# Expert weights in a hybrid SSD / gMLP / MoE step: chunks of one row step of both experts, and extra steps taken row by row in the doubled pair

## The reference

```
for each expert e:                      # w_gu[e] 1024 x 2048, w_down[e] 1024 x 1024, all float32
    gu = x[tokens of e] @ w_gu[e] + b_gu[e]
    act = glu * sigmoid(1.702 * glu) * (lin + 1)      # glu, lin: clamped even and odd columns
    y[tokens of e] += gate * (act @ w_down[e] + b_down[e])
```

## Time and profile before

| | us |
|---|---|
| runs of the kernel before | 1468.93, 1472.8, 1466.63 (median 1468.93) |
| the profiled execution's own time | 1467.76 |
| its span, first to last instruction | 1465.6 |
| PE busy in the span | 1389.4 (95%) |
| packets of the SP queue, share of 16 DMA engines | 77.7% |
| mean granted TensorE clock | 0.99 |

### The profile page before, as it was taken

One profiled execution on the slowest core, in us unless ns is written; L12 is line 12 of the kernel. 1 busy time (PEld: TensorE's weight loads), 2 busy tenths in 40 slices (PEclk: granted clock), 3 DMA queues, 4 the chain that ended last, 5 costly groups with the idle time before them and its releaser, 6 DMA issues.

```text
span 1465.6 us, 21942 instructions
## 1 busy us (share of the span) xinstructions
PE 1389.4 (95%) x8524; PEld 815.9 (56%) x8525; DVE 585.9 (40%) x1304; ACT 381.3 (26%) x643; POOL 206.9 (14%) x305
## 2 busy tenths in 40 slices
PE   7999999999999999999899899999999989889996
PEld 6998888888999444434434345343443443434432
DVE  6788887877443254312312123131221231212214
ACT  5557777766322241001001000010100100100002
POOL 4034454536810000000000000000000000000000
PEclk9999999999999999999999999999999999999999
DMA  8434555555454789999999999999999999999996
GB/s 263 133 121 151 150 178 153 173 169 147 158 158 144 316 344 386 428 429 429 428 428 429 429 428 426 429 427 386 424 428 428 429 428 429 429 428 428 428 424 235
DMA packets 124889, 482.91 MB, mean 330 GB/s; under 512 B 7197, under 2 KB 95325, under 8 KB 99929
## 3 DMA queue, kind: packets, MB, share of 16 engines
q1 hardware_dynamic: 86752, 459.16, 77.7%
q10 hardware_dynamic: 35904, 18.88, 4.4%
q0 software_dynamic: 2160, 3.87, 0.8%
HBM read 470.55 MB, written 11.34 MB: 329 GB/s over the span
## 4 chain that ended last, share of the span: by engine, by line
PE 69%; DMA 23%; DVE 3%; ACT 2%; issue 1%; SPq 1%; POOL 1%; ACTq 0%; POOLq 0%; DVEq 0%
DMA ring_b<-in_w_gu 19%; PE bank L1482 18%; PE bank L1688 11%; PE bank L1291 8%; PE bank L970 4%; PE bank L961 4%; PE bank L1409 4%; PE bank L942 3%; DMA ring<-in_w_gu 3%; PE bank L966 2%; PE bank L963 2%; PE bank L1520 2%; PE bank L1310 2%; PE bank L1200 1%; PE bank L1570 1%
## 5 line engine op out<-in xcount | busy, mean ns | idle before, releaser
L1482 PE MATMUL bank<-ring_b,xe 128*64 128x512 f32 x1168 | 324.1, 613 | 38.2 <-DMA ring_b<-in_w_gu 30.0
L1482 PEld LDWEIGHTS bank<-ring_b,xe 128*64 128x64 f32 x1168 | 103.7, 141 | 234.3 <-issue 233.5
L1482 PE MATMUL bank<-ring,xe 128*64 128x512 f32 x720 | 215.5, 596 | 3.1 <-DMA ring<-in_w_gu 3.1
L1688 PE MATMUL bank<-ring,actT 128*64 128x512 f32 x672 | 198.6, 595 | 0.0
L1821 ACT ACTIVATE swi<-swi 128x256 f32<-128x256 f32 x65 | 27.0, 417 | 549.0 <-DVE swi L2805 518.2
L2846 DVE TENSOR_TENSOR hid<-hid,bank 128x512 f32<-128x512 f32 (+1 forms) x90 | 57.7, 681 | 225.6 <-PE bank L1434 207.8
L1291 PE MATMUL bank<-rounded,ring_r 128*128 128x320 f32 x912 | 133.7, 307 | 1.7 <-DVE ring_r L2628 1.7
L1291 PEld LDWEIGHTS bank<-rounded,ring_r 128*128 128x128 f32 x912 | 132.8, 188 | 2.6 <-DVE ring_r L2628 2.4
L914 POOL TENSOR_TENSOR kept<-take 128x256 bf16<-128x256 bf16 x15 | 9.2, 612 | 829.6 <-PE bank L1670 829.6
L1482 PEld LDWEIGHTS bank<-ring,xe 128*64 128x64 f32 x720 | 68.4, 137 | 64.7 <-issue 64.7
L1688 PE MATMUL bank<-ring_b,actT 128*64 128x512 f32 x224 | 98.7, 594 | 4.0 <-ACT actT L2204 4.0
(11 more groups left out here) (421 smaller groups left out, 2026.6 us busy)
## 6 DMA issues: line engine op xcount, KB each, us to landing
ring_b<-in_w_gu SPq DMA_DIRECT2D x76, 2048.0 KB, 16.6
ring<-in_w_gu SPq DMA_DIRECT2D x48, 2048.0 KB, 16.7
ring<-in_w_down SPq DMA_DIRECT2D x45, 2048.0 KB, 18.1
ring<-in_w_in SPq DMA_DIRECT2D x32, 1024.0 KB, 5.4
ring_b<-in_w_down SPq DMA_DIRECT2D x15, 2048.0 KB, 15.8
arena<-in_state_ssm ACTq DMA_DIRECT2D x16, 512.0 KB, 4.9
out<-arena ACTq DMA_DIRECT2D x16, 512.0 KB, 3.6
ring<-in_w_branch_ssd SPq DMA_DIRECT2D x8, 1024.0 KB, 5.1
```

Of the source, the lines that this page charges most:

```text
L1482: mm = pe.matmul(bank[q][side(h), :], xe[:, j, side(h)], moe_slot(2 * i + h, first)[:, 2 * FF * k + 512 * q:2 * FF * k + 512 * q + 512], s ...
L1688: mm = pe.matmul(bank[4 + half][side(h), :], actT[:, f, side(h)], w[:, D * k + 512 * half:D * k + 512 * half + 512], start=False, stop=(f ...
```

## The change

A chunk still has 2 MB and a pair still has twelve, but a chunk of `w_gu` is now one row step of both experts, and a chunk of `w_down` two steps f of both. It is loaded by two DMAs of 1 MB, each of 2048 consecutive floats (8 KB) in 128 partitions, `PIECE` floats apart in the slot. PE waits for one chunk at each row step and gives it back at its end. In the doubled pair, the extra steps of rows 0 and 1 stay together; from row 2 to row 5 each row step is followed at once by its extra step; the extra steps of rows 6 and 7 come after row 7. Chunks there are given back after the extra step. In the last pair only chunks 10 and 11 are still special, and keep their layout (`LAST_WHOLE` = 10).

```diff
-LAST_WHOLE = 2 * GU_CHUNKS - 2
+LAST_WHOLE = PAIR_CHUNKS - 2
+PIECE = GU_ROWS * FF
 def pair_chunk_ready(pe, n, c, more16, first=False):
-            count = n * 32 + (filled[s] + 16 * (c // MOE_RING + 1))
+            count = n * 64 + (filled[s] + 32 * (c // MOE_RING + 1))
 ...
-            def load_chunk(c, e, j, first=False):
-                    sp.dma_start(dst, gu_t[j][:, bass.ds(e, 1), :].rearrange("p e n -> p (e n)")
+            def load_chunk(c, experts, first=False):
+                rows_t, i = (gu_t, c) if c < KD else (down_t, c - KD)
+                at = slice(PIECE * (i % 2), PIECE * (i % 2) + PIECE)
+                for h in range(2):
+                    sp.dma_start(dst[:, PIECE * h:PIECE * h + PIECE],
+                                 rows_t[i // 2][:, bass.ds(experts[h], 1), at].rearrange("p e n -> p (e n)")
+                                 ).then_inc(full, 16)
 ...
 def gate_up(...):
-                    elif k == 0:
-                        for h in range(2):
-                            pair_chunk_ready(pe, n, 2 * i + h, more16, first)
+                    pair_chunk_ready(pe, n, j, more16, first)
                     for q in range(4):
                         for h in range(2):
 ...
-                            if q == 3 and k == GU_ROWS - 1:
-                                mm.then_inc(chunk_used, 1)
+                    mm.then_inc(chunk_used, 1)
 def gate_up_double(n):
-                for i in range(GU_CHUNKS):
-                    both(2 * i)
-                    both(2 * i + 1)
-                    if i < 3:
-                        combine(n - 1, i)
-                    if i == 0:
+                for j in range(KD):
+                    both(j)
+                    if j in (1, 3, 5):
+                        combine(n - 1, j // 2)
+                    if j == 1:
 ...
-                    more_slots(2 * i)
-                    more_slots(2 * i + 1)
+                        more_slots(0)
+                    if 1 <= j < KD - 2:
+                        more_slots(j)
+                more_slots(KD - 2)
+                more_slots(KD - 1)
 def down_double(n):       # more_slots(j), four steps f
-                    mm.then_inc(chunk_used, 1)
+                        if f % 2 == 1:
+                            mm.then_inc(chunk_used, 1)
```

More of the change, by code:

```diff
@@ L1455, in combine_last, with gate_up @@
                               start=False, stop=True).then_inc(S["cm_psum"], 1)
[L1457 removed]
+            def gate_up(n, more16, first=False, before_it=False, extras=None, double=False, inputs=False):
                 if first:
@@ L1560, in both @@
                 def both(f):
[L1562 to L1566, removed]
+                    if f % 2 == 0:
+                        pair_chunk_ready(pe, n, KD + f // 2, None)
+                    if f % DOWN_ROWS == 0:
+                        pe.wait_ge(S["at_ready"], 2 * n + (f // DOWN_ROWS + 1))
                     for half in range(2):
                         for h in range(2):
[L1569 to L1574, removed]
+                            pe.matmul(bank[4 + half][side(h), :], actT[:, f, side(h)], down_row(f, h, half),
+                                      start=False, stop=(f == KD - 1))
                 def more_slots(j):
-                    for k in range(DOWN_ROWS):
-                        f = DOWN_ROWS * j + k
+                    for f in range(DOWN_ROWS * j, DOWN_ROWS * j + DOWN_ROWS):
                         for half in range(2):
[L1581 to L1584, removed]
+                            mm = pe.matmul(bank[3][quarter(2 * half + f % 2), :], actT_extra[:, f, :],
+                                           down_row(f, 1, half), start=(f == 1), stop=(f >= KD - 2))
+                        if f % 2 == 1:
+                            mm.then_inc(chunk_used, 1)
                 for f in range(DOWN_ROWS):
@@ L1626, in down_last @@
                 turn_half(0)
[L1627 to L1631, removed]
-                        mm = pe.matmul(bank[4 + half][side(h), :], actT[:, f, side(h)],
-                                       w[:, D * k + 512 * half:D * k + 512 * half + 512],
-                                       start=False, stop=(f == KD - 1))
-                    return mm
                 pe.wait_ge(S["at_ready"], 2 * n + 1)
                 for piece in range(2):
-                    for h in range(2):
-                        last_piece_ready(pe, 2 * GU_CHUNKS + h, piece, more16)
+                    pair_chunk_ready(pe, n, KD + piece, more16)
                     for f in (2 * piece, 2 * piece + 1):
                         for half in range(2):
-                            mm = down_step(f, half)
+                            for h in range(2):
+                                mm = pe.matmul(bank[4 + half][side(h), :], actT[:, f, side(h)], down_row(f, h, half),
+                                               start=False, stop=False)
                     mm.then_inc(chunk_used, 1)
@@ L1653, in down_last @@
                     for h in range(2):
-                        last_piece_ready(pe, 2 * (GU_CHUNKS + 1) + h, half, more16)
+                        last_piece_ready(pe, LAST_WHOLE + h, half, more16)
                     for f in range(DOWN_ROWS, KD):
-                        mm = down_step(f, half)
+                        at = D * (f - DOWN_ROWS) + 512 * half
+                        for h in range(2):
+                            mm = pe.matmul(bank[4 + half][side(h), :], actT[:, f, side(h)],
+                                           moe_slot(LAST_WHOLE + h)[:, at:at + 512], start=False, stop=(f == KD - 1))
                     mm.then_inc(chunk_used, 1)
@@ L1676, in down @@
                 for f in range(KD):
-                    j, k = f // DOWN_ROWS, f % DOWN_ROWS
-                    if k == 0:
-                        for h in range(2):
-                            pair_chunk_ready(pe, n, 2 * (GU_CHUNKS + j) + h, more16, first)
+                    if f % 2 == 0:
+                        pair_chunk_ready(pe, n, KD + f // 2, more16, first)
                     if f % 4 == 0:
@@ L1686, in down @@
                         for h in range(2):
-                            w = moe_slot(2 * (GU_CHUNKS + j) + h, first)
-                            mm = pe.matmul(bank[4 + half][side(h), :], actT[:, f, side(h)],
-                                           w[:, D * k + 512 * half:D * k + 512 * half + 512],
+                            mm = pe.matmul(bank[4 + half][side(h), :], actT[:, f, side(h)], down_row(f, h, half, first),
                                            start=False, stop=(f == KD - 1))
-                            if k == DOWN_ROWS - 1 and half == 1:
-                                mm.then_inc(chunk_used, 1)
+                    if f % 2 == 1:
+                        mm.then_inc(chunk_used, 1)
                     if f == 3 and first:
@@ L1810, in _ @@
                 block_of(n, more * 16, extras=more)
-            gate_up(NP - 1, more * 16, before_it=True, last=True, extras=more)
+            gate_up(NP - 1, more * 16, before_it=True, extras=more)
             down_last(more * 16)
```

99 lines of the change are left out of this document (40 added, 59 removed).

## The result

The changed kernel takes 1474.61 us in the median of 12 runs (1473.32 to 1478.96), the kernel before 1468.88 (1466.63 to 1472.82, 12 runs). The ratio is 1.0043, with a 95% interval of 1.0034 to 1.0052: some 6 us slower, within the 0.5% that was named as no telling change, though the interval shows that it is not zero. The profiled execution has a span of 1471.9 us, against 1465.6.

What follows compares the result with a forecast made beforehand. Transfers, not PE, were taken to set the pace: 192 chunks plus a tail. +13.0 - 3.55 - 4.4, with 0 for the ends, gave +5.05 us on the median 1468.93: forecast 1474 (chance 0.54), range 1464 to 1486.

Steps and rivals of the forecast that it cites:

- term 3: Doubled pair: the stream's stop for lack of free slots goes away with finer give-backs, -4.4 us.
- Term 1: Steady stream: 8 KB loads lower the rate to 422 GB/s, 0.0755 us more for each of 172 chunks, +13.0 us.
- Rivals A: Stream rate: it costs more, 417 GB/s, +23.2 - 8 = +15, 1484, slower; chance 0.24.
- C: Steady stage: 8 KB costs nothing, rate stays at 428 GB/s, -8 us, 1461, faster; chance 0.10.
- rival D: Stream: each added DMA leaves the engines idle for a moment; 0.3 us of it would give 1518; chance 0.01.
- Term 2: Start: an earlier give-back in pair 0 lets chunk 2 of pair 1 issue sooner, -3.55 us.
- Term 4: The ends: loads ahead of the router, the last pair's halves and all behind the last landing change nothing, 0.
- Rival B: Doubled pair: it keeps its gap, give-back too late or PE not ahead, +9.5 us, 1478.4, slower; chance 0.11.

Runs made afterwards that it cites:

- e1: Kernel before, each chunk loaded by two DMAs of 8 KB runs, waits and give-backs untouched: 1477.9 us, ratio 1.0076.
- e3: Kernel before, each w_gu chunk in one DMA with two 8 KB runs per partition, row steps reordered: 1475.05 us, ratio 1.0043.
- e10: Changed kernel with pair 0 back in one-expert chunks (one DMA, 16 KB runs): 1477.71 us, ratio 1.0064 to the kernel before.
- e5: Kernel before with only pair 0 in row-step chunks of both experts (two DMAs, 8 KB runs): 1467.1 us, ratio 1.000.
- e4: Changed kernel with the old order of extra steps in the doubled pair: 1475.16 us, ratio 1.0046 to the kernel before.
- e7: Changed kernel, row-step chunks only in pairs 0, 7, 8 and from row 6 of the last; 16 KB runs elsewhere: 1467.79 us, 0.9993 to the kernel before.
- e8: Changed kernel, row-step chunks only in pairs 0, 1, 6, 7, 8 and from row 6 of the last: 1465.6 us, 0.9979 to the kernel before.
- e2: Kernel before, each chunk loaded by two DMAs of 64 partitions, runs still 16 KB: 2162.3 us, no ratio given.

## Why the prediction was right

**The size and the sign.** 1474 was predicted and 1474.61 measured. That it is so close is partly luck: term 3 earned 1.0 us less than forecast and 1.0 us was lost at a place that had been put at nothing, while the medians lie only 0.7 us further apart than forecast (5.7 against 5.05).

**Term 1, +13.0, held.** 422 GB/s in all windows of whole pairs, 4.970 us a chunk in the chain, from eight halves of the last pair. e1 shows that it is the runs of the load and not the new waits, e3 that it is their length and not the number of DMAs. Rivals A (417) and C (428) fall, and with them D. The Trainium skill's numbers for a single DMA of 1 MB (DMA: Bandwidth & Descriptors, Bandwidth) played no part in a queue that is never empty: 186 more DMAs left no cost that is seen beside that of the runs. The "over +1200 us" of the prediction takes the Trainium skill's 6.15 us for one DMA of 1 MB (same page and section). By the 341 GB/s of the same row two of 1 MB take 6.15 us together, and the sum would be about +210 us, an estimate from that row. Nothing of either size came.

The 1518 of rival D does not follow from its 0.3 us, since 172 x 0.3 is 51.6 us: 1526 on top of the forecast, or 1513 in place of its rate. Nothing else rests on it.

**Term 2, -3.55, held as the changed kernel has it** (3.59 in the traces of e10 and of the changed kernel). But its reason was incomplete. I took it as a property of pair 0 alone. (567.71, which it gave for the issue of chunk 2, is that of chunk 3, but the sum uses the give-back at 567.35.) e5 shows that it also takes pair 1's give-backs by row, or a stream that is slower: with whole chunks behind it the stream loses 2.0 us again.

**Term 3, -4.4, was 1.0 us too large, and most of what it earned comes with the slower stream alone.** Between the landings at row 5 of pair 6 and row 7 of pair 9 lie 38 chunks. The kernel before takes 190.98 us for them, 5.0 over full rate. The changed kernel takes 1075.86 - 885.33 = 190.53, which is 1.6 over 38 x 4.970 = 188.9. So 3.4 are gained, not 4.4. In e1, with the old give-backs, the chain has the same two landings:

```profile
889.31 7.09 PE bank L1487 x32
...
1080.59 7.11 PE bank L1487 x32
```

191.28, only 2.4 over full rate. So with the slower stream taken first, 2.6 of the 3.4 us come from it, which asks for its slots later, and 0.8 from finer chunks. No run has finer chunks there without the lower rate, so the shares in the other order are open. A stop of a stream that waits for PE is a part of PE's time, and any slowing of the stream fills it first. I had named this (the give-backs hardly move in pair 7), but did not take it for the main cause.

**Term 4, nothing at the ends, missed 1 us in the last pair.** From row 7 of pair 9 to the last landing the kernel before takes 373.18 us and the changed one 379.42, so 6.24 more, where term 1 has 70 x 0.0755 = 5.3. The chain of the changed kernel from row 7 of pair 14 on, and the last landing of the kernel before:

```profile
1374.10 3.65 PE bank L1473 x16
...
1424.82 3.68 PE bank L1473 x16
...
1440.82 14.46 DMA ring<-in_w_down
```

```profile
1435.10 13.89 DMA ring<-in_w_down
```

From 1374.10 to row 5 of pair 15 at 1424.82 are ten chunks, which take 50.72 us instead of 49.70. The two other kernels with fine chunks at the start of the last pair have this too (51.17 in e4, 50.63 in e10), e1 has not (49.89). Why this landing is late is open.

**The sum.** Counted from the first row step of pair 0, the landing at row 5 of pair 6 comes 0.92 us later than in the kernel before (1.3 by terms 1 and 2), the 38 chunks of term 3 take 0.45 less (1.5 forecast), and the rest takes 6.24 more (5.3). That makes +6.7, less 0.4 by which the mixer ended earlier in this execution: 6.3, the difference of the two spans. The medians differ by 5.7.

**Rival B and DVE.** Rival B (the gap stays) did not come, but its place was rightly named: e7 and e8 have the stop there. DVE's later `swiglu` was hidden, as said; its idle time before the next work fell from 2.64 us to 1.62 in the changed kernel:

```profile
965.84 1.29 DVE L2826 TENSOR_TENSOR xe<-bank,nf_pairs 128x512 f32<-128x512 f32 x2 [1.62 <-PE bank L1405]
```

## What to carry to other kernels

Where transfers bound a stage, first ask what a change does to the rate of every transfer, and only then what it does to waits: 1.5% of the rate over 172 chunks outweighed two gaps closed. The price was to be had beforehand, from a few transfers of the same shape at the end of the old trace. Gaps in a stream are not independent terms: a stream that comes earlier meets the next late give-back, and a slower one fills gaps by itself; so finer chunks belong where the ring is full (here pairs 0 and 1, 0.2% faster) and long runs everywhere else.

## What the runs showed of the hardware

**Half of the partitions, half of the rate for most of the time.** DMAs of 64 partitions with 16 KB runs, one after the other on one queue, moved 215 GB/s at a DMA share of 1.01 (e2, 640 to 880 us), where 128 partitions moved 428; later in the same execution they reached 304. The time grew by 36% in the fastest of the four runs and by 57% in the slowest.

**The length of the runs counts even at 8 KB.** 16 KB per partition gave 428 GB/s and 8 KB 422, in one DMA (e3, by its mixture of 424) or in two (e1).

**The granted clock of TensorE no longer fell.** In the kernel before PE idled 2.71 us for a landing at 1369.70 and was then granted 1.2 GHz instead of 2.4 for some 3 us, as in a few other pairs. These are PE's instructions there, and a window:

```profile
1369.70 4.89 PE L1482 MATMUL bank<-ring_b,xe 128*64 128x512 f32 x13 [2.71 <-DMA ring_b<-in_w_gu]
```

```profile
1370.00:1374.00 4.00, 4.00 (x13) 1.37 (x11) 0.00 (x0) 0.00 (x0) 0.00 (x0) 0.57 1.01 430
```

In the changed kernel PE waits in shorter pieces, mostly of 1.3 us or less, and the windows from 640 to 880 and from 1060 to 1400 show a granted clock of 1.00. No gain is seen from it: the DMA share in these windows is 1.01 in either kernel, and PE waits for the stream.
